# Last output products cut in two around the probability transposes, and another order of the small steps at the two layer borders

## The chip, the cores and the metric

The kernel runs on one core of a Trainium2 chip. The metric is the device time of one execution in microseconds (us). The core's engines are named as in the profile: PE is TensorE (PEld its weight loads), DVE is VectorE, ACT is ScalarE, POOL is GpSimd; SP issues most of the transfers, and its queue is written SPq.

## What is computed

Two blocks of a small network over 512 positions of width 1024. The first block runs two layers over 16 + 512 rows; `l` is 0 or 1.

```python
for l in range(2):
    a, g, zc, q, k, v, za, qi, ki, wi = split(h @ w_in[l])
    y_conv = gated depthwise convolution of (a, g), layer norm, silu, times silu(zc)
    y_attn = attention over the 132 keys that score best by (qi, ki, wi), times silu(za)
    y = concat(y_conv, y_attn) @ w_out[l]
    h = layer_norm(ALPHA * h + y) * post_ln_g[l] + post_ln_b[l]
x = rmsnorm(h, norm_gain)            # second block: one layer
q, k, v, gate_a, u, v_in, gate_b, merge = split(x @ w_in_2)
...                                  # attention, gated MLP, merge, output product, last norm
```

## The kernel before

**Numbers.** Every large product is made of three passes over a high and a low part: `x_hi` times `w_hi`, `x_lo` times `w_hi`, `x_hi` times `w_lo`. ACT makes a high part by a copy that rounds; a low part is what the rounding left. Low parts of the activations are subtractions on DVE (`x_lo(l, t)` for row tile t) or on POOL (`part_low`); low parts of the weights come by ACT and an accumulating transfer that POOL issues (`split_lo`), or, for the blocks in `LO_BY_POOL`, by two subtractions on POOL (`subtract_hi`, one for each half of the block).

**Weights.** They stream in blocks of 128x2048 through a ring of four buffers. SP loads block n when the last product that uses block n-4 has been made; then ACT splits it, then its low part is made. In the second block the ring's order is kv, q (two blocks), vin (two blocks), u (two), and so on: vin's second block takes kv's place, so its load waits for the last kv product, `("kv", 3)`.

**Rows.** Tiles 0 (16 rows) and 1 to 4 (128 rows each). In a layer's attention PE takes pairs of heads in turn, tile by tile; item i is one tile and one head. For each item PE transposes the probabilities (`turn_probs`, into one bank of `psum_A`, its last 16 keys into `psum_B` for tile 4), ACT copies them out (`take_probs_t`), and PE multiplies them by v (`probs_times_v`). Other work is put between these by tables: `OUTPUT_AT` names the items at which the output product of a finished tile is made (24 matmuls: 12 for the convolution half, 12 for the attention half), `POST_AT` those at which its layer norm is made.

**Border.** After the last item PE makes the output product of tile 4 in four parts (its two column halves `n`, the convolution half by `output_conv`, the attention half by `output_attn`) and, between them, transposes the finished tiles for the next layer (`turn_rows`). The norm of tile 4 runs last: DVE `residual(l, 1, 4)`, `aggregate`, then POOL `ln_deviation`, then DVE `post_norm`. After layer 1 comes the input norm of the second block as well: ACT squares the rows, POOL `input_deviation`, DVE `second_input(t)` scales them into `h_normed`, PE `turn_rows(1, t)` transposes them, ACT `x_hi` and DVE `x_lo` take them. The second block starts with the products `("kv", t)` (24 matmuls of 256 columns) and the halves `("q", t, half)` (12 matmuls of 512 columns), in the order of `KV_AND_Q`; `x_ready(1, t + 1)` makes `("kv", t)` wait for `x_lo(1, t + 1)`. Each engine works its instructions in the order in which they are written.

Of the kernel before, what the change touches and what calls it, by code (L numbers as in the profile page):

```python
# [26 lines left out]
P = 128  # L27
D = 1024
# [211 lines left out]
def gate_needed(l, name, t):  # L240
# [21 lines left out]
OUTPUT_CONV_AT = {0: 38, 1: 30}  # L262
# [6 lines left out]
KV_AND_Q = (("kv", 0), ("kv", 1), ("kv", 2), ("q", 0, 0), ("kv", 3), ("q", 1, 0), ("q", 2, 0), ("q", 3, 0),  # L269
# [27 lines left out]
def attention_extras(l):  # L297
# [51 lines left out]
    todo["pe"][OUTPUT_CONV_AT[l]].append(("wo conv", 0))  # L349
# [36 lines left out]
def build(nc, io, counted):  # L386

    with ExitStack() as ctx:
# [69 lines left out]
        hn = [sb("h_normed0", [P, D], at=K_AT + 4 * D), sb("h_normed1", [P, D], at=where[0])]  # L458
# [690 lines left out]
        def _(pool):  # L1149
            def subtract_hi(n):  # L1150

                for half in range(2):
# [65 lines left out]
            for l in range(DEPTH):  # L1218
# [55 lines left out]
                subtract_hi(after + 1)  # L1274
                ln_deviation((l, "post", 4), 4, P)
                split_lo(after + 2)
# [48 lines left out]
        def _(pe):  # L1325
# [229 lines left out]
            def output_half(l, n, half, t, ps):  # L1555
# [6 lines left out]
                for kk in range(4):  # L1562
# [15 lines left out]
            def output_conv(l, n):  # L1578
                buf, at = OUTPUT_BANK[n]
                ps = claim((l, "wo", n, 4), buf, (at,))[:, 0, :]  # L1580
                output_half(l, n, 0, 4, ps).then_inc(psum_full.mark((l, "wo", n, 4, "conv")), 1)
# [8 lines left out]
            for l in range(DEPTH):  # L1590
# [76 lines left out]
                def woven(i):  # L1667
                    for op in todo[i]:
# [8 lines left out]
                        elif op[0] == "wo":  # L1677
                            output_rows(l, *op[1:])
                        else:
                            output_conv(l, *op[1:])  # L1680
# [3 lines left out]
                for i in range(0, n, 2):  # L1684
# [7 lines left out]
                    woven(i + 1)  # L1692
                probs_times_v(l, n - 2)
# [110 lines left out]
            for name, t, *half in KV_AND_Q:  # L1804
                if name == "kv":
# [3 lines left out]
                    if t == 2:  # L1809
                        turn_rows(1, 4)  # L1810
                else:
                    query_half(t, *half)
            turn["AB"] = 1
# [44 lines left out]
        def _(dve):  # L1858
# [290 lines left out]
            for l in range(DEPTH):  # L2149
# [43 lines left out]
                for i in range(0, n, 2):  # L2193
# [12 lines left out]
                    woven(i + 1)  # L2206
                y_part(l, "attn", 4)

                if l < DEPTH - 1:
                    x_lo(l, 0)  # L2210
                    x_lo(l, 1)
                else:
                    second_input(1)
                    second_input(2)
                    x_lo(l, 1)
                    second_input(3)
                    x_lo(l, 2)
                residual(l, 0, 4)
                if l < DEPTH - 1:
                    x_lo(l, 2)  # L2220
                x_lo(l, 3)
# [3 lines left out]
                if l == DEPTH - 1:  # L2225
                    second_input(4)
                x_lo(l, 4)
# [339 lines left out]
```

## Time and profile before

| | |
|---|---|
| median of 3 runs | 1025.12 us (1024.62 to 1025.96) |
| the profiled execution | 1024.52 us, of it the span of the trace 1022.6 us |
| PE busy | 987.3 us, 97% of the span |
| DVE, ACT, POOL busy | 667.8, 558.8 and 231.4 us |
| mean granted clock of TensorE | 0.993 of full speed |

The span runs from the first to the last instruction. PE's busy time is nearly all of it; what is left to gain by order alone is the time in which PE waits, and a wait that another work covers costs nothing. The profile names for each wait the instruction that ended it.

### The profile page before, as it was taken

How to read it: one execution, taken by the hardware profiler on the slowest of the kernel's cores; microseconds unless marked ns; L12 is line 12 of the kernel's file. 1: busy time of each engine (PE TensorE's matmuls, PEld its weight loads, DVE VectorE, ACT ScalarE, POOL GpSimd, SP SyncE). 2: the span in 40 equal slices, each digit the busy share in tenths (PEclk: the TensorE clock that was granted, in tenths of full speed). 3: DMA queues.
4: the chain of work that ended last, by engine and by line, in shares of the span. 5: the costliest groups of instructions: out<-in, count | busy, mean ns of one | idle time of the engine just before them, and what ended most of it. 6: DMA issues, size and time to landing. Idle time of an engine off the chain costs nothing.

```text
span 1022.6 us, 15789 instructions
## 1 busy us (share of the span) xinstructions
PE 987.3 (97%) x6084; PEld 816.8 (80%) x6084; DVE 667.8 (65%) x1439; ACT 558.8 (55%) x915; POOL 231.4 (23%) x250
## 2 busy tenths in 40 slices
PE   7999999998999999999999999999999999999997
PEld 7888988886677988888778677888888788888886
DVE  3899999888674489999988756638422333333432
ACT  6685891645333558588165534544646566564442
POOL 0110771115211401077111512634101000000001
PEclk9999999999999999999999899999999999999999
DMA  8876874752001577488464400577777536365662
GB/s 301 196 180 179 210 181 131 166 124 83 1 1 50 157 177 176 124 185 187 124 171 79 156 21 1 171 180 188 176 210 197 114 89 158 90 158 126 175 155 82
DMA packets 23098, 143.92 MB, mean 141 GB/s; under 512 B 2785, under 2 KB 3297, under 8 KB 7281
## 3 DMA queue, kind: packets, MB, share of 16 engines
q0 software_dynamic: 8496, 60.36, 31.7%
q1 hardware_dynamic: 14528, 82.55, 22.8%
q8 instruction: 49, 0.80, 0.3%
q14 instruction: 25, 0.20, 0.1%
HBM read 140.81 MB, written 2.10 MB: 140 GB/s over the span
## 4 chain that ended last, share of the span: by engine, by line
PE 81%; ACT 7%; DVE 5%; DMA 3%; POOL 2%; issue 2%; SPq 0%; POOLq 0%; DVEq 0%; ACTq 0%
PE psum_B L1371 21%; PE psum_A L1371 14%; PE psum_B L1406 7%; PE psum_A L1406 7%; PE psum_A L1568 6%; PE psum_C L1448 3%; PE psum_A L1786 2%; PE psum_B L1568 2%; PE psum_B L1786 2%; PE psum_A L1484 2%; PE psum_B L1512 2%; DVE conv_acc L1887 2%; POOL w_lo L1155 2%; PE psum_B L1773 2%; PE psum_C L1371 1%
## 5 line engine op out<-in xcount | busy, mean ns | idle before, releaser
L1162 POOL DMA_DIRECT2D w_lo<-in_weights x59 | 52.0, 881 | 562.2 <-ACT w_lo L706 536.0
L1887 DVE SCALAR_TENSOR_TENSOR conv_acc<-u,vec,conv_acc 128x528 f32<-128x528 f32 (+1 forms) x240 | 172.3, 755 | 3.2
L1371 PE MATMUL psum_B<-x_hi,w_hi 128*128 128x264 f32 (+3 forms) x472 | 143.9, 338 | 2.5 <-DVE mlp_lo L2341 1.2
L1371 PE MATMUL psum_B<-x_lo,w_hi 128*128 128x264 f32 (+3 forms) x472 | 141.7, 333 | 0.0
L1371 PE MATMUL psum_B<-x_hi,w_lo 128*128 128x264 f32 (+3 forms) x472 | 141.2, 332 | 0.0
L705 ACT ACTIVATE w_hi<-w_raw 128x2048 fp32r<-128x2048 f32 (+2 forms) x73 | 113.4, 1553 | 18.7 <-DMA w_raw<-in_weights 18.2
L1371 PE MATMUL psum_A<-x_hi,w_hi 128*128 128x264 f32 (+3 forms) x408 | 111.1, 311 | 2.0 <-DVE za L2041 0.9
L706 ACT ACTIVATE w_lo<-w_raw 128x2048 fp32r<-128x2048 f32 (+2 forms) x73 | 112.7, 1544 | 0.0
L1371 PE MATMUL psum_A<-x_lo,w_hi 128*128 128x264 f32 (+3 forms) x408 | 109.1, 306 | 0.0
L1371 PE MATMUL psum_A<-x_hi,w_lo 128*128 128x264 f32 (+3 forms) x408 | 109.0, 305 | 0.0
L1371 PEld LDWEIGHTS psum_B<-x_hi,w_hi 128*128 128x128 f32 (+1 forms) x472 | 82.1, 186 | 13.4 <-issue 3.7
L1371 PEld LDWEIGHTS psum_B<-x_hi,w_lo 128*128 128x128 f32 (+1 forms) x472 | 82.0, 187 | 8.9
L1371 PEld LDWEIGHTS psum_B<-x_lo,w_hi 128*128 128x128 f32 (+1 forms) x472 | 82.0, 186 | 8.2
L1371 PEld LDWEIGHTS psum_A<-x_hi,w_hi 128*128 128x128 f32 (+1 forms) x408 | 70.0, 186 | 7.9 <-issue 3.1
L1371 PEld LDWEIGHTS psum_A<-x_hi,w_lo 128*128 128x128 f32 (+1 forms) x408 | 70.0, 186 | 3.4
L1371 PEld LDWEIGHTS psum_A<-x_lo,w_hi 128*128 128x128 f32 (+1 forms) x408 | 70.0, 186 | 3.4
L1946 DVE MATCH_REPLACE8 score<-top,score 128x528 f32<-128x528 f32 (+2 forms) x102 | 56.0, 557 | 0.0
L1937 DVE MAX8 top<-score 128x8 f32<-128x528 f32 (+2 forms) x102 | 51.6, 560 | 1.2 <-POOL score L1231 1.2
L1406 PE MATMUL psum_A<-w_hi,x_hi 128*128 128x512 f32 (+1 forms) x128 | 49.0, 383 | 0.5 <-ACT shifted L764 0.4
L1406 PE MATMUL psum_B<-w_hi,x_hi 128*128 128x512 f32 (+1 forms) x128 | 48.9, 382 | 0.4 <-ACT shifted L764 0.4
L1406 PE MATMUL psum_B<-w_hi,x_lo 128*128 128x512 f32 (+1 forms) x128 | 48.7, 380 | 0.0
L1406 PE MATMUL psum_A<-w_hi,x_lo 128*128 128x512 f32 (+1 forms) x128 | 48.7, 380 | 0.0
(407 smaller groups left out, 2199.5 us busy)
## 6 DMA issues: line engine op xcount, KB each, us to landing
w_raw<-in_weights SPq DMA_DIRECT2D x66, 1024.0 KB, 5.0
w_lo<-in_weights POOLq DMA_DIRECT2D x57, 1024.0 KB, 8.6
h<-in_x SPq DMA_DIRECT2D x1, 2048.0 KB, 11.0
out<-h SPq DMA_DIRECT2D x4, 512.0 KB, 2.6
x_first<-in_x_t SPq DMA_DIRECT2D x3, 528.0 KB, 8.3
post_ln_g<-in_post_ln_g SPq DMA_DIRECT2D x2, 512.0 KB, 4.7
post_ln_b<-in_post_ln_b SPq DMA_DIRECT2D x2, 512.0 KB, 6.1
w_raw<-in_weights SPq DMA_DIRECT2D x2, 288.0 KB, 6.4
```

The source lines that it names most:

```text
L705: act.activation(whi[n % RING][:, a:b], raw[n % RING][:, a:b], ACT.Copy)
L706: got = act.activation(wlo[n % RING][:, a:b], raw[n % RING][:, a:b], ACT.Copy, scale=-1.0)
L1155: pool.tensor_tensor(wlo[n % RING][:, a:b], raw[n % RING][:, a:b], whi[n % RING][:, a:b].bitcast(F32), ALU.subtract).then_inc(pool_lo.mark ...
L1162: pool.dma_start(wlo[n % RING][:, 0:width], io["weights"][n, :, 0:width], accum_op=ALU.add) \
L1371: mm = pe.matmul(ps[0:cols, i, 0:b - a], w[wp][:, kt, at:at + cols], x[xp][:, kt, a:b], start=(kt == 0 and wp + xp == 0), stop=(kt == KD - ...
L1406: mm = pe.matmul(ps[:, 0, 0:width], act_parts[xp][:, kt, c0:c0 + P], w[wp][:, kk, at:at + width], start=(kt == 0 and wp + xp == 0), stop=( ...
L1448: mm = pe.matmul(banks[odd][0:SIZE[t], i, 0:b - a], qs[s:s + HD, hd // 2, START[t]:END[t]], ks_of[s:s + HD, a:b], start=True, stop=True)
L1568: mm = pe.matmul(ps, x[xp][:, kt, START[t]:START[t] + P], w[wp][:, kk, 0:DC], start=(kt == 0 and wp + xp == 0), stop=(kt == KD - 1 and wp ...
L1786: mm = pe.matmul(ps[:, 0, :], w[wp][:, kt, d % 4 * P:d % 4 * P + P], parts[xp][:, kt, :], start=(kt == 0 and wp + xp == 0), stop=(kt == CT ...
L1887: got = dve.scalar_tensor_tensor(dst, src, w, dst, ALU.mult, ALU.add)
L1937: dve.max(top8[:, t - 1, :], vals).then_inc(topk_max.mark((l, r, t)), 1)
L1946: dve.match_replace(vals, top8[:, t - 1, :], vals, MARK).then_inc(topk_marked.mark((l, r, t)), 1)
```

## The change

Three edits, none of which adds or takes away arithmetic; the POOL subtraction of one weight block is issued as two separate steps with another step between them.

1. In the last four items of each layer's attention, the output product of tile 3's second column half, 24 matmuls in one piece before, is made in two pieces of 12, one on each side of a probability transpose, and the product `wo conv 0` of tile 4, 12 matmuls in one piece before, in two pieces of 6 around the last one.
2. At both borders DVE makes the low part of tile 3 (`x_lo(l, 3)`), and after layer 1 that of tile 2 too, later in its order; `residual` and the norm of tile 4 come ahead. POOL makes the deviation for tile 4 between the two halves of the second weight block. After layer 1 the scaled inputs of tiles 1 and 2 (`second_input`) come ahead of the last gated attention tile (`y_part`), for which `h_normed` is given other memory (that of `k`).
3. In `KV_AND_Q`, `("kv", 3)` goes behind two more query halves, and the transpose of tile 4 behind `("q", 0, 0)` instead of behind `("kv", 2)`.

```diff
-        (34, 0, 3, "A"), (36, 1, 3, "A")),
+        (34, 0, 3, "A")),
...
-OUTPUT_CONV_AT = {0: 38, 1: 30}
+LAST_OUTPUT_AT = {0: 36, 1: 28}
...
-KV_AND_Q = (("kv", 0), ("kv", 1), ("kv", 2), ("q", 0, 0), ("kv", 3), ("q", 1, 0), ("q", 2, 0), ("q", 3, 0),
+KV_AND_Q = (("kv", 0), ("kv", 1), ("kv", 2), ("q", 0, 0), ("q", 1, 0), ("q", 2, 0), ("kv", 3), ("q", 3, 0),
...
-    todo["pe"][OUTPUT_CONV_AT[l]].append(("wo conv", 0))
+    i = LAST_OUTPUT_AT[l]
+    todo["pe"][i].append(("wo rows", 0, 1, 3, "A"))
+    todo["pe"][i + 1].append(("wo rows", 1, 1, 3, "A"))
+    todo["dve"][i + 1].append(("residual", 1, 3))
+    todo["pe"][i + 2].append(("wo conv", 0, 0, 2))
+    todo["pe"][i + 3].append(("wo conv", 0, 2, 4))
...
-        hn = [sb("h_normed0", [P, D], at=K_AT + 4 * D), sb("h_normed1", [P, D], at=where[0])]
+        hn = [sb(f"h_normed{i}", [P, D], at=K_AT + 4 * D * i) for i in range(2)]
...
-            def subtract_hi(n):
+            def subtract_hi(n, parts=(0, 1)):
 
-                for half in range(2):
+                for half in parts:
...
                 subtract_hi(after)
-                subtract_hi(after + 1)
+                subtract_hi(after + 1, (0,))
                 ln_deviation((l, "post", 4), 4, P)
+                subtract_hi(after + 1, (1,))
                 split_lo(after + 2)
...
+            def output_part(l, half, n, t, buf):
+
+                use = (l, "wo", n, t)
+                ps = (bank[buf][:, 1:2, :] if half else claim(use, buf, (1,)))[:, 0, :]
+                mm = output_half(l, n, half, t, ps)
+                if half:
+                    mm.then_inc(psum_full.mark(use), 1)
...
-                    if t == 2:
-                        turn_rows(1, 4)
                 else:
                     query_half(t, *half)
+                    if (t, *half) == (0, 0):
+                        turn_rows(1, 4)
...
+                if l == DEPTH - 1:
+                    second_input(1)
+                    second_input(2)
                 y_part(l, "attn", 4)
 
                 if l < DEPTH - 1:
                     x_lo(l, 0)
-                    x_lo(l, 1)
                 else:
-                    second_input(1)
-                    second_input(2)
-                    x_lo(l, 1)
                     second_input(3)
-                    x_lo(l, 2)
+                x_lo(l, 1)
                 residual(l, 0, 4)
-                if l < DEPTH - 1:
-                    x_lo(l, 2)
-                x_lo(l, 3)
+                x_lo(l, 2)
                 residual(l, 1, 4)
                 aggregate(l, 4)
                 post_norm(l, 4)
                 if l == DEPTH - 1:
                     second_input(4)
+                x_lo(l, 3)
                 x_lo(l, 4)
```

The order of instructions shows it at three places; the line numbers in the rows of the change are its own. First PE, at the last probability transpose of layer 1 (`exps_124` are the probabilities, `w_hi_51` and `w_lo_59` the weights of `wo conv 0`), before:

```order
L1568 MATMUL psum_A<-w_hi_51,x_hi 128x512
L1568 MATMUL psum_A<-w_hi_51,x_lo 128x512
L1568 MATMUL psum_A<-w_lo_59,x_hi 128x512
L1484 MATMUL psum_A<-ident,exps_124 128x128 x4
L1490 MATMUL psum_B<-ident,exps_124 16x64
L1512 MATMUL psum_B<-probs_t_113,v 64x128
```

and with the change:

```order
L1577 MATMUL psum_A<-w_hi_51,x_hi 128x512
L1577 MATMUL psum_A<-w_hi_51,x_lo 128x512
L1577 MATMUL psum_A<-w_lo_59,x_hi 128x512
L1493 MATMUL psum_A<-ident,exps_124 128x128 x4
L1499 MATMUL psum_B<-ident,exps_124 16x64
L1577 MATMUL psum_A<-w_hi_51,x_hi 128x512
L1577 MATMUL psum_A<-w_hi_51,x_lo 128x512
L1577 MATMUL psum_A<-w_lo_59,x_hi 128x512
```

Six of the product's matmuls now stand between the transpose and the first product with v; the other places of this kind look the same.

Second DVE, at the border to the second block, from the first residual of tile 4 on (tile 3 stands in `psum_D`, tiles 2 and 4 in `psum_C`), before:

```order
L2080 SCALAR_TENSOR_TENSOR h<-h,psum_A 128x512
L2088 BN_STATS stats<-h 128x6
L2127 TENSOR_TENSOR x_lo<-psum_D,x_hi 128x8x128
L2080 SCALAR_TENSOR_TENSOR h<-h,psum_B 128x512
L2088 BN_STATS stats<-h 128x6
L2093 BN_AGGR meanvar<-stats 128x2
L2103 SCALAR_TENSOR_TENSOR h<-h,meanvar,post_ln_g 128x1024
L2107 SCALAR_TENSOR_TENSOR h<-h,rstd,post_ln_b 128x1024
L2119 SCALAR_TENSOR_TENSOR h_normed_99<-h,rstd,norm_gain 128x1024
L2127 TENSOR_TENSOR x_lo<-psum_C,x_hi 128x8x128
```

and with the change:

```order
L2102 SCALAR_TENSOR_TENSOR h<-h,psum_A 128x512
L2110 BN_STATS stats<-h 128x6
L2149 TENSOR_TENSOR x_lo<-psum_C,x_hi 128x8x128
L2102 SCALAR_TENSOR_TENSOR h<-h,psum_B 128x512
L2110 BN_STATS stats<-h 128x6
L2115 BN_AGGR meanvar<-stats 128x2
L2125 SCALAR_TENSOR_TENSOR h<-h,meanvar,post_ln_g 128x1024
L2129 SCALAR_TENSOR_TENSOR h<-h,rstd,post_ln_b 128x1024
L2141 SCALAR_TENSOR_TENSOR h_normed_99<-h,rstd,norm_gain 128x1024
L2149 TENSOR_TENSOR x_lo<-psum_D,x_hi 128x8x128
L2149 TENSOR_TENSOR x_lo<-psum_C,x_hi 128x8x128
```

The low part of tile 3, from `psum_D`, moved from ahead of the second residual to behind the scaled input of tile 4.

Third POOL, at the same border (`w_lo_59` is kv's low part, `w_lo_60` that of the first query block, `w_lo_57` that of the second), before:

```order
L1155 TENSOR_TENSOR w_lo_59<-w_raw_55,w_hi_51 128x1024 x2
L1155 TENSOR_TENSOR w_lo_60<-w_raw_56,w_hi_52 128x1024 x2
L1171 TENSOR_SCALAR var_eps<-meanvar 128x1
L1174 TENSOR_TENSOR rstd<-var_eps,minus_half 128x1
L1162 DMA w_lo_57<-in_weights 128x2048
L1171 TENSOR_SCALAR var_eps<-prob_sums 128x1
```

and with the change:

```order
L1163 TENSOR_TENSOR w_lo_59<-w_raw_55,w_hi_51 128x1024 x2
L1163 TENSOR_TENSOR w_lo_60<-w_raw_56,w_hi_52 128x1024
L1179 TENSOR_SCALAR var_eps<-meanvar 128x1
L1182 TENSOR_TENSOR rstd<-var_eps,minus_half 128x1
L1163 TENSOR_TENSOR w_lo_60<-w_raw_56,w_hi_52 128x1024
L1170 DMA w_lo_57<-in_weights 128x2048
L1179 TENSOR_SCALAR var_eps<-prob_sums 128x1
```

The second half of the query block's subtraction moved behind the first deviation, and so ahead of the transfer and of the second deviation (`var_eps<-prob_sums`), which still stand behind it.

## Rows read from the trace of the kernel before

**Rows 1.** The page, busy time, share of the span and instructions of each engine

```profile
PE 987.3 (97%) x6084; PEld 816.8 (80%) x6084; DVE 667.8 (65%) x1439; ACT 558.8 (55%) x915; POOL 231.4 (23%) x250
```

**Rows 2.** Timeline of PE: start us, us, instruction [idle before, its releaser]

```profile
319.30 0.63 PE L1484 MATMUL psum_A<-ident,exps 128*128 128x128 f32 x4 [0.83 <-ACT probs_t L846]
...
325.85 0.33 PE L1512 MATMUL psum_B<-probs_t,v 128*64 128x128 f32 x2 [0.78 <-ACT probs_t_meta L846]
...
649.28 1.07 PE L1552 MATMUL psum_C<-ident,h_normed 128*128 128x128 f32 x8 [0.54 <-DVE h_normed L2119]
```

**Rows 3.** Timelines of POOL, DVE and PE at the first border

```profile
337.69 4.78 POOL L1155 TENSOR_TENSOR w_lo<-w_raw,w_hi 128x1024 fp32r<-128x1024 f32 x2 [2.52 <-ACT w_hi L702]
342.55 1.11 POOL L1171 TENSOR_SCALAR var_eps<-meanvar 128x1 f32<-128x1 f32 x1
...
339.50 1.23 DVE L2127 TENSOR_TENSOR x_lo<-psum_C,x_hi 128x1024 fp32r<-128x1024 f32 x1 [1.58 <-ACT x_hi L889]
...
344.41 1.28 DVE L2107 SCALAR_TENSOR_TENSOR h<-h,rstd,post_ln_b 128x1024 f32<-128x1024 f32 x1 [0.80 <-POOL rstd L1174]
...
345.84 1.07 PE L1552 MATMUL psum_D<-ident,h 128*128 128x128 f32 x8 [0.77 <-DVE h L2107]
```

**Rows 4.** Timeline of DVE at the second border

```profile
650.09 1.23 DVE L2127 TENSOR_TENSOR x_lo<-psum_D,x_hi 128x1024 fp32r<-128x1024 f32 x1 [0.95 <-ACT x_hi L889]
...
656.86 0.68 DVE L2080 SCALAR_TENSOR_TENSOR h<-h,psum_B 128x512 f32<-128x512 f32 x1
...
658.30 0.21 DVE L2093 BATCH_NORM_AGGREGATE meanvar<-stats 128x2 f32<-128x12 f32 x1
...
661.38 1.28 DVE L2107 SCALAR_TENSOR_TENSOR h<-h,rstd,post_ln_b 128x1024 f32<-128x1024 f32 x1 [0.80 <-POOL rstd L1174]
664.97 1.28 DVE L2119 SCALAR_TENSOR_TENSOR h_normed<-h,rstd,norm_gain 128x1024 f32<-128x1024 f32 x1 [2.30 <-POOL rstd L1174]
```

**Rows 5.** Timelines of POOL and ACT at the second border

```profile
648.28 11.21 POOL L1155 TENSOR_TENSOR w_lo<-w_raw,w_hi 128x1024 fp32r<-128x1024 f32 x4 [0.23 <-ACT w_hi L702]
659.58 1.05 POOL L1171 TENSOR_SCALAR var_eps<-meanvar 128x1 f32<-128x1 f32 x1
...
662.06 0.91 POOL L1162 DMA_DIRECT2D w_lo<-in_weights  x1 [0.80 <-ACT w_lo L706]
663.95 0.18 POOL L1171 TENSOR_SCALAR var_eps<-prob_sums 128x1 f32<-128x1 f32 x1 [0.97 <-ACT square L899]
...
662.70 1.06 ACT L899 ACTIVATE square<-h 128x1024 f32<-128x1024 f32 x1 [0.99 <-DVE h L2107]
```

**Rows 6.** Timeline of PE at the second border: first kv matmul, transpose of tile 4

```profile
656.62 0.28 PE L1406 MATMUL psum_A<-w_hi,x_hi 128*128 128x256 f32 x1
...
666.40 1.06 PE L1552 MATMUL psum_C<-ident,h_normed 128*128 128x128 f32 x8 [1.12 <-DVE h_normed L2119]
```

**Rows 7.** Chain that ended last: start us, us, what (a whole kv product)

```profile
670.25 2.82 PE psum_B L1406 x24
```

**Rows 8.** Timelines around vin's second weight block, and vin's first matmul

```profile
673.10 0.33 SPq L618 DMA_DIRECT2D w_raw<-in_weights  x1
...
681.70 1.92 ACT L705 ACTIVATE w_hi<-w_raw 128x2048 fp32r<-128x2048 f32 x1 [8.15 <-DMA w_raw<-in_weights]
...
685.78 0.91 POOL L1162 DMA_DIRECT2D w_lo<-in_weights  x1 [8.08 <-ACT w_lo L706]
...
692.36 0.40 PE L1406 MATMUL psum_A<-w_hi,x_hi 128*128 128x512 f32 x1
```

**Rows 9.** Transfers issued from 685.6 to 698: count, KB, median us to landing

```profile
w_lo<-in_weights POOLq DMA_DIRECT2D x1, 1024.0 KB, 7.9
```

**Rows 10.** Stretches: length, busy PE, PEld, DVE, ACT, POOL, PEclk, DMA share, GB/s

```profile
577.00:582.00 5.00, 5.00 (x16) 3.21 (x17) 4.89 (x14) 2.49 (x7) 1.12 (x4) 0.50 0.68 223
1016.00:1019.00 3.00, 0.46 (x2) 0.02 (x1) 1.44 (x3) 0.85 (x3) 0.74 (x2) 1.00 0.06 23
1019.00:1020.00 1.00, 0.00 (x0) 0.00 (x0) 0.43 (x1) 0.59 (x1) 0.00 (x0) 0.54 0.00 0
```

More of the change, by code:

```diff
@@ L253 @@
     0: ((17, 0, 0, "A"), (19, 0, 1, "B"), (22, 1, 0, "A"), (25, 1, 1, "B"), (27, 0, 2, "A"), (29, 1, 2, "A"),
[2 rows of a table removed]
+        (34, 0, 3, "A")),
+    1: ((17, 0, 1, "A"), (19, 0, 2, "B"), (21, 1, 1, "A"), (23, 1, 2, "A"), (26, 0, 3, "A")),
 }
@@ L1553, in turn_rows, with output_half @@
                 mm.then_inc(psum_full.mark(use), 1)
-            def output_half(l, n, half, t, ps):
+            def output_half(l, n, half, t, ps, kks=range(4)):
                 part = ("conv", "attn")[half]
@@ L1561, in output_half @@
                     pe.wait_ge(meta_paired.sem, meta_paired.at((l, part)))
-                for kk in range(4):
+                for kk in kks:
                     kt = half * 4 + kk
@@ L1576, in output_rows, with output_conv @@
                 output_half(l, n, 1, t, ps).then_inc(psum_full.mark(use), 1)
-            def output_conv(l, n):
+            def output_part(l, half, n, t, buf):
[4 more added lines that the diff above has]
+                    mm.then_inc(psum_full.mark(use), 1)
+            def output_conv(l, n, first=0, last=4):
                 buf, at = OUTPUT_BANK[n]
-                ps = claim((l, "wo", n, 4), buf, (at,))[:, 0, :]
-                output_half(l, n, 0, 4, ps).then_inc(psum_full.mark((l, "wo", n, 4, "conv")), 1)
+                ps = (bank[buf][:, at:at + 1, :] if first else claim((l, "wo", n, 4), buf, (at,)))[:, 0, :]
+                mm = output_half(l, n, 0, 4, ps, range(first, last))
+                if last == 4:
+                    mm.then_inc(psum_full.mark((l, "wo", n, 4, "conv")), 1)
             def output_attn(l, n):
@@ L1678, in woven @@
                             output_rows(l, *op[1:])
+                        elif op[0] == "wo rows":
+                            output_part(l, *op[1:])
                         else:
```

1 row of the table OUTPUT_AT is left out of this document.

## Prediction

> **What bounds the kernel now.** I read the page first: PE is busy 987.3 us of a span of 1022.6 [rows 1], so only its waits, some 35 us, can be won by another order, and a new wait of PE is paid in full wherever PE has no later idle time to give it up in. Then the waits of PE near the edits, in its timeline. At the last item of a layer's attention PE transposes probabilities, and the next transpose or product waits until ACT has copied them out: 0.83 us at 319.30, 0.78 at 325.85 [rows 2]; the same pair stands in layer 1, so there are four such waits. The transpose of tile 2 waits 0.54 for DVE's `h_normed` [rows 2], the transpose of tile 4 at the first border 0.77 for the norm [rows 3], and at the second border 1.12 for `h_normed` of tile 4 [rows 6]. These waits are what the edits can take away. Against them stands what the moved steps released before: whom did `x_lo(1, 3)` and `("kv", 3)` let go, and when? Those I read from the timelines of DVE, POOL and SP at the second border.
>
> **Edit 1, pieces around the transposes.** No matmul is added. After each of these transposes PE now has 12 matmuls or 6 of them; the shorter piece, at the kv block's rate of 2.82 us for 24 narrower matmuls [rows 7] no faster than 0.7 us and by its doubled columns about 1.4, covers waits of 0.83 and 0.78. Gain 4 x 0.8 = 3.2 us, half in each layer. What the pieces wait for (bank, probabilities) was there long before. Bounds: 2.6 if pieces restart slowly, 3.2.
>
> **Edit 2 at the first border.** `x_lo(0, 3)`, 1.23 us, stood ahead of the second residual, and POOL's deviation started at 342.55 only after both halves of the subtraction, 4.78 us from 337.69 [rows 3]. With both out of the way the norm of tile 4 comes up to 1.3 us earlier, and the 0.77 us of PE's wait goes. The delayed second half of the weight subtraction (2.4 us, half of 4.78) now starts after the deviation, at about the same distance to its user; it may cost up to 0.5. I take 0.7. Bounds 0.2 to 0.9.
>
> **Edit 2 at the second border, the start.** The scaled inputs of tiles 1 and 2 come while DVE idles, and the 0.54 of [rows 2] goes. But the transpose of tile 3 needs `x_lo(1, 1)`, which ended at 651.32 [rows 4], and that hangs on ACT and on kv's weights, whose load starts no earlier. PE would reach it at about 651, so little is left of it: I take 0.05, bounds 0 to 0.5. With edit 1 the last product of tile 4 ends 1.65 us earlier in layer 1's own time.
>
> **Edit 2 at the second border, the new wait.** `("kv", 2)` waits for `x_lo(1, 3)`, which now stands behind `second_input(4)`. When is that? Before, the second residual started at 656.86 and the aggregate ended at 658.51 [rows 4]; the deviation started at 659.58, 1.07 late, behind POOL's subtractions (four in 11.21 us, 2.8 each) [rows 5]. Now the residual starts at 656.86 - 1.65 = 655.2, the aggregate ends at 656.9, three subtractions end at 648.28 + 8.4 = 656.7. Deviation and root took 661.38 - 659.58 = 1.8 with the way to DVE [rows 4, 5], so the norm's last step runs 658.7 to 660.0 and the square ends at 661.2. POOL meanwhile makes the fourth subtraction, 658.6 to 661.4, and issues the transfer, 0.91 [rows 5], to 662.4; then the second deviation, 664.97 - 663.95 = 1.0, to 663.4: the 1.2 us that POOL's order costs here cancels the 1.07 won. `second_input(4)` 1.28 to 664.7, `x_lo(1, 3)` 1.23 to 665.95, PE at 666.0. PE is ready for `("kv", 2)` after two kv products: 656.62 - 1.65 + 2 x 2.82 = 660.6 [rows 6, 7]. So it waits 5.4 us, in place of 1.12 at the transpose of tile 4, which is now long ready. Bounds: 4.2 (POOL never in the way) to 6.2.
>
> **Edit 3, the ring.** `("kv", 3)` moves behind two query halves more (the transpose of tile 4 stays ahead of it). Seven query halves took 692.36 - 673.07 = 19.3 us after it, 2.76 each [rows 7, 8]. SP issued the load of vin's second block when it was done, 673.10; ACT split it at 681.70, POOL issued the low part at 685.78, and it landed 7.9 later, 693.7 [rows 8, 9]: 20.6 us after `("kv", 3)`. The first vin product needs it for its second half, 2.8 us after its start: 22.1 after `("kv", 3)`, so 1.5 to spare. With the change only five query halves follow: 13.8 + 2.8 = 16.6, and the low part is 4.0 us late. Nothing behind it gives this back: the loads that follow hang on PE's own products. Bounds 0.5 (the load, 8.6 us beside another, as if alone by 3.5 faster) to 7 (the low part beside the loads that the last query half lets go).
>
> **The clock.** In this trace, with TensorE idle from 1016.5, the granted clock was still 1.00 until 1019 and 0.54 in the next microsecond; from 577 to 582, after sparse work, it stood at 0.50, the lower level of 1.2 GHz, with PE busy all 5 us [rows 10]. A wait of 5.4 us is longer than that idle stretch. Work at half speed for 5 us costs 2.5; I take 2.0 for the kv wait, bounds 0 and 2.5, and none for the 4.0 us wait, in which the forecast is near even. The Trainium skill, TensorE: Matmul & The Clock Gate, section "HAM oscillation — how this bites in real kernels", says that a TensorE left waiting for a transfer is throttled back and works its next matmuls cold, every time. By that rule both new waits would cost it, and the sum would be 2.0 us higher; the trace agrees with the fall after idling, and no row shows one after a wait of PE of 4 us inside the kernel.
>
> **The sum**, against the profiled execution's 1024.52: -3.2 (transposes), -0.7, -0.05, +5.4 - 1.1 (kv wait for the tile 4 wait), +2.0 (clock), +4.0 (vin) = +6.35; 1030.9. The median of the runs is 0.6 above that execution: 1031.5.
>
> **The rivals.**
> - The clock falls at the vin wait too: 1033.5. For it: 4.0 us of idling against some 3 at the end [rows 10]. Against: PE works 12 matmuls just before. 20%.
> - The clock never falls: 1029.5. For it: the three rows are all there is, and none shows a fall after one long wait inside the kernel. Against: the kv wait is almost twice the idle stretch at the end. 12%.
> - Only the kv wait is real, because vin's low part lands in time: 1025.5 to 1027.5 with the clock's share. It needs the 20.6 us chain to shrink to 16.6; the contended load could give 3.5. 14%.
> - Faster: `x_lo(1, 3)` is there when PE asks. Then 3.2 + 0.75 + 1.1 are won and vin's wait must be absent too: 1020. It decides at 660.6: if the chain from the residual to `x_lo(1, 3)` took under 5.5 us instead of 10.8. Its DVE and ACT steps alone (0.68, 0.69, 0.21, 1.28, 1.06, 1.28, 1.23) take 6.4. 6%, mostly for an error of mine in who waits for whom.
>
> **How the numbers follow.** My forecast, both waits and one fall of the clock, has 40%, its own range 1029 to 1034. The rest, 8%, are other costs of either sign. The range for 8 in 10 is 1026.8 to 1035: it leaves out the faster case, part of the third, and the high tail of the vin wait with a second fall. A measurement of this kernel tells about 0.2% from no change, 2.05 us. Faster 7%, the same 8% (the lower half of the third rival and some of the rest), slower 85%.
>
> **What would show it.** In the changed kernel's trace: no wait on `probs_t` before the last transposes and products of each layer; none before the transpose of tile 4 at the first border; on PE a wait of 4 to 6 us ahead of the third kv product that ends with `x_lo`; a PEclk near 0.5 just after it; a wait of 2.5 to 5 us in the middle of the first vin product that ends with the transfer into `w_lo`; from there to the end the same durations as before. I am wrong if the kv wait is under 3 us, if the vin product runs through, or if later waits of PE shrink and give the time back.

## The result and the profile after

The changed kernel takes 1038.53 us (median; 1035.53 to 1040.48) against 1024.87 us of the kernel before: a ratio of 1.0127, 95% interval 1.0115 to 1.0139, or 13.7 us slower. The forecast was 1031.5 us, and its range ended at 1035.0. The profiled execution, at 1035.53 us the shortest of the four, is 11.0 us above that of before.

The page's busy row answers to [rows 1]; columns as there.

```profile
span 1033.5 us, 15791 instructions
## 1 busy us (share of the span) xinstructions
PE 990.4 (96%) x6084; PEld 819.2 (79%) x6084; DVE 670.3 (65%) x1439; ACT 558.3 (54%) x915; POOL 229.2 (22%) x250
```

PE has the same 6084 matmuls and is busy 3.1 us longer; the other 7.8 us of the longer span are time in which it waits. The waits of PE around the two borders, 318 to 360 and 640 to 715 us (who waits, for whom, sum, number, longest):

```profile
PE psum_D L1561 <- DVE h L2129: 1.5, 1, 1.5
PE psum_C L1561 <- DVE x_lo L2149: 0.7, 1, 0.7
...
PE psum_A L1415 <- DVE x_lo L2149: 6.2, 1, 6.2
PE psum_A L1415 <- DMA w_lo<-in_weights: 3.4, 1, 3.4
PE psum_D L1561 <- DVE x_lo L2149: 1.3, 1, 1.3
```

The waits on `probs_t` (two of them in [rows 2]) are gone. The first row is the 0.77 of [rows 3], grown to 1.48 where the forecast had it vanish; the two of 0.7 and 1.3 on `x_lo` are new and were not forecast; the kv wait of 6.2 and the wait of 3.4 for vin's `w_lo` are the two that were.

The first border after, DVE, POOL and PE (timelines; they answer to [rows 3]):

```profile
340.07 1.28 DVE L2125 SCALAR_TENSOR_TENSOR h<-h,meanvar,post_ln_g 128x1024 f32<-128x1024 f32 x1
342.15 3.32 DVE L2129 SCALAR_TENSOR_TENSOR h<-h,rstd,post_ln_b 128x1024 f32<-128x1024 f32 x1 [0.80 <-POOL rstd L1182]
...
340.12 1.28 POOL L1179 TENSOR_SCALAR var_eps<-meanvar 128x1 f32<-128x1 f32 x1 [1.83 <-DVE meanvar L2115]
341.49 0.55 POOL L1182 TENSOR_TENSOR rstd<-var_eps,minus_half 128x1 f32<-128x1 f32 x1
342.00 2.39 POOL L1163 TENSOR_TENSOR w_lo<-w_raw,w_hi 128x1024 fp32r<-128x1024 f32 x1
...
345.62 1.06 PE L1561 MATMUL psum_D<-ident,h 128*128 128x128 f32 x8 [1.48 <-DVE h L2129]
```

POOL's deviation now starts 2.43 us earlier than in [rows 3] (340.12 for 342.55), as the edit means it to, and the norm's last step on DVE 2.26 earlier. But this step, 1.28 us in [rows 3], shows 3.32, and it ends 1.08 behind the subtraction half that POOL began just before it (342.00 + 2.39 = 344.39, 345.47). The step ends where it ended before, and PE's transpose of tile 4 starts at 345.62 for 345.84.

The second border after, DVE, POOL and PE (they answer to [rows 4 to 6]):

```profile
659.88 3.32 DVE L2129 SCALAR_TENSOR_TENSOR h<-h,rstd,post_ln_b 128x1024 f32<-128x1024 f32 x1 [0.79 <-POOL rstd L1182]
665.50 1.28 DVE L2141 SCALAR_TENSOR_TENSOR h_normed<-h,rstd,norm_gain 128x1024 f32<-128x1024 f32 x1 [2.30 <-POOL rstd L1182]
666.70 1.21 DVE L2149 TENSOR_TENSOR x_lo<-psum_D,x_hi 128x1024 fp32r<-128x1024 f32 x1
...
657.85 1.28 POOL L1179 TENSOR_SCALAR var_eps<-meanvar 128x1 f32<-128x1 f32 x1 [1.65 <-DVE meanvar L2115]
...
659.73 2.38 POOL L1163 TENSOR_TENSOR w_lo<-w_raw,w_hi 128x1024 fp32r<-128x1024 f32 x1
...
655.90 0.28 PE L1415 MATMUL psum_A<-w_hi,x_hi 128*128 128x256 f32 x1
...
667.97 0.58 PE L1415 MATMUL psum_A<-w_hi,x_hi 128*128 128x256 f32 x1 [6.25 <-DVE x_lo L2149]
```

The same pair stands here: 3.32 us beside POOL's 2.38. The kv block starts only 0.72 before that of [rows 6], and its third product waits 6.25.

Vin's second block (timelines of ACT, POOL and PE, as [rows 8]):

```profile
691.61 1.92 ACT L713 ACTIVATE w_hi<-w_raw 128x2048 fp32r<-128x2048 f32 x1 [6.71 <-DMA w_raw<-in_weights]
...
695.69 0.91 POOL L1170 DMA_DIRECT2D w_lo<-in_weights  x1 [9.10 <-ACT w_lo L714]
...
698.16 0.39 PE L1415 MATMUL psum_A<-w_hi,x_hi 128*128 128x512 f32 x1
...
704.53 0.50 PE L1415 MATMUL psum_A<-w_hi,x_hi 128*128 128x512 f32 x1 [3.44 <-DMA w_lo<-in_weights]
...
708.99 0.39 PE L1415 MATMUL psum_B<-w_hi,x_hi 128*128 128x512 f32 x1
```

SP issued the load at 684.45, when `("kv", 3)` was done; the low part was there at 704.5, 20.1 later. And the clock (stretches, columns as [rows 10]):

```profile
664.00:665.00 1.00, 0.00 (x0) 0.00 (x0) 0.00 (x0) 1.00 (x6) 0.44 (x2) 0.52 0.61 98
...
668.00:672.00 4.00, 4.00 (x23) 4.00 (x24) 0.00 (x0) 0.00 (x0) 0.00 (x0) 0.64 0.93 304
672.00:675.00 3.00, 3.00 (x17) 2.44 (x16) 0.00 (x0) 0.45 (x2) 0.00 (x0) 1.00 0.03 12
702.00:705.00 3.00, 0.47 (x2) 0.42 (x3) 2.93 (x12) 0.00 (x0) 2.83 (x3) 1.00 0.94 330
705.00:708.00 3.00, 3.00 (x9) 2.31 (x8) 2.96 (x9) 0.00 (x0) 1.10 (x1) 0.50 0.99 421
```

The granted clock, the seventh number, is at 0.5, the level of 1.2 GHz, from about 664 on, with PE idle since 661.7, and again from 705, just behind the wait of 3.44 us. It costs 1.41 at the kv product (667.97 to the next product at 672.20 is 4.23, against 2.82 in [rows 7]; the lower level began while PE still stood, so over half of it cost nothing) and 1.68 at vin (12 matmuls in 708.99 - 704.53 = 4.46, against 2.78, half of a vin product of before).

The 10.9 us by which the span is longer, by place, as the shift of PE's starts against before, in the two profiled executions:

| PE reaches | before | after | shift | change |
|---|---|---|---|---|
| the product behind layer 0's last transposes | 327.29 | 325.42 | -1.87 | -1.87 |
| layer 1's first block behind tile 4's transpose | 346.66 | 346.66 | 0 | +1.87 |
| transposes of tile 1, second border | 647.71 | 646.23 | -1.48 | -1.48 |
| transposes of tile 2 | 649.28 | 647.10 | -2.18 | -0.70 |
| first kv product | 656.62 | 655.90 | -0.72 | +1.46 |
| third kv product | 662.28 | 667.97 | +5.69 | +6.41 |
| first vin product | 692.36 | 698.16 | +5.80 | +0.11 |
| second vin product | 697.92 | 708.99 | +11.07 | +5.27 |
| the end | 1022.6 | 1033.5 | +10.9 | -0.2 |

Not all of the first -1.87 is the change's. At 300 us, ahead of every edited place, PE is already 0.38 early: before, the granted clock is at 0.50 from 242 to 244 us, and in this execution it is at 1.00 there. The pieces around the transposes give the other 1.5.

### The profile page after: what moved, and what is told of

The parts are those of the page before. It is cut to its first block, busy times and chain, and to the rows that moved or that the text cites. A ratio compares the mean times of both kernels' runs of the same rounds, so it can differ in the third digit from the quotient of the medians.

```text
span 1033.5 us, 15791 instructions
## 1 busy us (share of the span) xinstructions
PE 990.4 (96%) x6084; PEld 819.2 (79%) x6084; DVE 670.3 (65%) x1439; ACT 558.3 (54%) x915; POOL 229.2 (22%) x250
## 4 chain that ended last, share of the span: by engine, by line
PE 81%; ACT 7%; DVE 6%; DMA 4%; issue 2%; POOL 0%; POOLq 0%; SPq 0%; DVEq 0%; ACTq 0%
PE psum_B L1380 21%; PE psum_A L1380 14%; PE psum_A L1415 8%; PE psum_B L1415 8%; PE psum_A L1577 6%; DMA w_raw<-in_weights 3%; PE psum_C L1457 2%; PE psum_B L1577 2%; PE psum_A L1808 2%; PE psum_B L1808 2%; DVE conv_acc L1909 2%; PE psum_A L1493 2%; PE psum_B L1521 2%; PE psum_B L1795 1%; PE psum_C L1380 1%
## 5 line engine op out<-in xcount | busy, mean ns | idle before, releaser
L1415 PE MATMUL psum_A<-w_lo,x_hi 128*128 128x512 f32 (+1 forms) x128 | 49.7, 388 | 0.0
```

What stands on the lines that cost most here:

```text
L1415: mm = pe.matmul(ps[:, 0, 0:width], act_parts[xp][:, kt, c0:c0 + P], w[wp][:, kk, at:at + width], start=(kt == 0 and wp + xp == 0), stop=( ...
```

## The experiments

Two theories of the miss stood at first. One: both forecast waits are there, a little larger, the clock falls at each, and POOL's new order costs what the transposes give. The rival: the waits forecast are the smaller part, and the loss is in transfers that come late and a clock that falls elsewhere. All ratios are to the kernel before on the same chip.

**The same kernel again.**

> The changed kernel once more, unaltered, for a second trace. Its four runs spread from 1035.53 to 1040.48 us with a granted clock of 0.990 down to 0.987. Theory A (the spread is the clock: after the two long waits of TensorE the lower level lasts for a different time in each run): the kv wait (6.2 us in the first trace) and the vin wait (3.4 us) are within 1 us of the first trace, and a time above 1036.5 comes with more microseconds at PEclk 0.50 behind them. Theory B (the spread is in transfers): the vin wait itself differs by 2 us or more.

1040.34 us (1039.15 to 1043.54), ratio 1.0153 (1.0133 to 1.0173). Its trace (1039.15) has the same kv wait, 6.25, and a wait for vin's low part of 5.15 in place of 3.44. The load was issued at 686.30, when `("kv", 3)` was done, and the product went on at 708.39, 22.1 us later, for 20.1 in the first trace. The vin wait differs by 1.7, so neither theory is met in full, and the trace has a share of each. Its span is 3.8 us longer: 1.8 of it come at the vin product, most of that the later transfer, 0.6 ahead of the kv block, and most of the rest with the clock. PE's busy time and granted clock there (length, PE busy, PEclk, DMA share, GB/s):

```profile
668.00:672.00 4.00, 3.43 (x16) 0.50 0.97 288
672.00:675.00 3.00, 3.00 (x14) 0.61 0.25 96
```

The kv wait ends at 668.57 here, and the lower level lasts to 674.3, where in the first trace it was over at 670.9, 2.9 after the wait's end: the kv product takes 5.28 instead of 4.23. The executions of this kernel spread over 8 us (1035.5 to 1043.5), those of before over 4.3 (1023.54 to 1027.83). Both the transfer and the place of the clock's fall have a part in that; how much of the 8 us each has, two traces can't show.

**POOL's order undone.** POOL again makes both halves, then the deviation.

```diff
-                subtract_hi(after + 1, (0,))
+                subtract_hi(after + 1)
                 ln_deviation((l, "post", 4), 4, P)
-                subtract_hi(after + 1, (1,))
```

> The change with POOL's order put back: both halves of the second block's subtraction ahead of the deviation for tile 4. Theory A (POOL's second half beside the norm's last step on DVE holds that step up, 3.32 us in place of 1.28, at both borders): the step is back at 1.28 in both places, the wait for it at the first border falls from 1.5 us to under 0.3, the kv wait from 6.2 to about 5, and the kernel is 2.5 to 3 us faster than the change (about 1035.5 beside 1038.5). Theory B (the prediction's: the order of POOL is neutral, the deviation would wait for the subtraction instead): within 1 us of the change.

1036.21 us (1033.94 to 1037.88), ratio 1.0101 (1.0084 to 1.0118), 4.1 us below the changed kernel on the same chip, where theory A gave 2.5 to 3. The norm's last step takes 1.28 at both borders, PE's wait for it at the first is gone, and the kv wait is 4.81 instead of 6.25. The norm's first step (L2124), which now runs in part beside POOL's last half, takes 1.68 and 1.87 instead of 1.28. The vin wait is 5.12 in this trace, so part of the gain went there.

**The place of `x_lo(1, 3)` undone**, ahead of the second residual as before, the rest of the change kept.

```diff
                 x_lo(l, 2)
+                if l == DEPTH - 1:
+                    x_lo(l, 3)
                 residual(l, 1, 4)
...
-                x_lo(l, 3)
+                else:
+                    x_lo(l, 3)
```

> The change with one step of DVE put back: after layer 1 the low part of tile 3 comes ahead of the second residual of tile 4 again. Theory A (the third kv product waits for it, and the clock falls in that wait): no wait of TensorE before the third kv product, none or under 0.5 us before the transpose of tile 4, no stretch at PEclk 0.50 there; the vin wait of 3.4 us stays, with a fall of the clock. 7 to 8 us faster than the change, some 1030.5. Theory B (that wait only takes the place of one for the scaled input of tile 4): a wait of over 3 us ahead of the transpose of tile 4 instead, and under 4 us faster.

1030.18 us (1027.43 to 1031.05), ratio 1.0039 (1.0025 to 1.0052): 10.2 us below the changed kernel, where theory A gave 7 to 8. No kv wait. The vin wait stands, 3.40 us, and the clock falls behind it.

**`KV_AND_Q` and the transpose of tile 4 undone**, the rest kept.

```diff
-KV_AND_Q = (("kv", 0), ("kv", 1), ("kv", 2), ("q", 0, 0), ("q", 1, 0), ("q", 2, 0), ("kv", 3), ("q", 3, 0),
+KV_AND_Q = (("kv", 0), ("kv", 1), ("kv", 2), ("q", 0, 0), ("kv", 3), ("q", 1, 0), ("q", 2, 0), ("q", 3, 0),
...
+                    if t == 2:
+                        turn_rows(1, 4)
...
-                    if (t, *half) == (0, 0):
-                        turn_rows(1, 4)
```

> The change with the order of kv and query products put back (the fourth kv product two query halves earlier, tile 4's transpose behind the third kv product). Theory A (the load of vin's second block hangs on the fourth kv product): the vin wait of 3.4 us is gone with the fall of the clock behind it, the kv wait of 6.2 us stays; 4.5 to 6 us faster than the change, some 1033. Theory B (the low part is late because the whole border is late and its transfer collides with others): a vin wait of over 2 us stays.

1031.79 us (1029.70 to 1033.13), ratio 1.0057 (1.0040 to 1.0075): 8.6 us below the changed kernel, where theory A gave 4.5 to 6. The vin wait is gone; the kv wait is 6.25 as before, with the clock's fall. So each forecast wait has its own cause, and either edit taken back removes its own. Both parts of the change that were forecast to lose do lose. All three runs gained more than theory A said. The three differences are against the changed kernel's second measurement, 1.0153; its first was 1.0127, so each is uncertain by 2.7 us.

**All three undone**: POOL's order, `x_lo(1, 3)`, `KV_AND_Q`. Left are the pieces around the transposes, `x_lo(0, 3)` behind the norm, and the scaled inputs ahead of the last gated tile.

> The changed kernel with three parts undone: the POOL order of the weight subtraction, the place of x_lo(1, 3) (again ahead of the second residual), and the place of ("kv", 3) with the transpose of tile 4. Kept: the pieces around the transposes, x_lo(0, 3) behind the norm, the second block's inputs ahead of the last gated tile. Theory A (each undone part made its own wait, and nothing else is in the change): no kv wait, no vin wait, no step of the norm above 2.3 us, the four transposes' waits gone; 1020.5 to 1022.5 against 1025.9. Theory B (what the transposes give is only moved to the next border, where POOL and DVE are the later ones): 1024 to 1026, with PE's waits for h or x_lo at the borders larger by what the transposes won.

1023.39 us (1021.88 to 1025.57), ratio 0.9987 (0.9978 to 0.9996), and later, measured anew,

> The best version so far once more, on the same chip as the one with the transpose of tile 4 moved. Theory A: 0.9978 to 0.9996 of before again, and 0.5 to 1 us above the one with the transpose moved. Theory B (the small gain was chance): within 0.1% of before.

1023.29 us (1021.58 to 1024.89), ratio 0.9981 (0.9972 to 0.9990). This version beats both kernels; it is 1.9 and 1.7 us faster than before, less than theory A gave it and more than B. Its waits at the second border, of the first of the two traces:

```profile
PE psum_D L1560 <- DVE x_lo L2148: 1.4, 1, 1.4
PE psum_C L1560 <- DVE h_normed L2140: 0.9, 1, 0.9
```

The 1.4 is the wait for `x_lo` of tile 1: PE is ready for the transpose of tile 3 that much ahead of ACT and DVE.

**The pieces around the transposes alone**, added to the kernel before.

> The kernel before with the pieces around the transposes alone. Theory A: 3 us less, 1022.9; the waits for the norm at the two borders stay near 0.8 and 1.1. Theory B (PE comes earlier to borders whose chain starts at POOL's or ACT's weight work and does not come earlier): the waits at the borders grow by 1 to 1.5 each and the kernel gains 0 to 1 us.

1026.35 us (1022.92 to 1031.00), ratio 1.0013 (1.0002 to 1.0025). Theory B, and more: the edit forecast at -3.2 is worth nothing by itself. The trace is of the longest execution (1031.0), so it shows how the edit can lose, and not what it does in the median. Its DVE and PE at the second border:

```profile
653.44 1.23 DVE L2148 TENSOR_TENSOR x_lo<-psum_D,x_hi 128x1024 fp32r<-128x1024 f32 x1 [4.65 <-ACT x_hi L897]
654.58 2.82 DVE L2140 SCALAR_TENSOR_TENSOR h_normed<-h,rstd,norm_gain 128x1024 f32<-128x1024 f32 x1
...
657.55 1.72 PE L1560 MATMUL psum_D<-ident,h_normed 128*128 128x128 f32 x7 [4.76 <-DVE h_normed L2140]
```

DVE stood 4.65 us for `x_hi`, which ACT made only at 652.41, behind two weight steps (650.50) that had waited 4.45 for their transfer. Then `h_normed` of tile 3, behind `x_lo(1, 1)` in the old DVE order, took 2.82 for 1.28, beside a subtraction of POOL (653.98 to 656.32). PE waited 4.76, and the clock fell. In the changed kernel `second_input(3)` is ahead of `x_lo(1, 1)`, and this wait is not there. How often it comes I can't say from one trace; the twelve executions lie from 1022.9 to 1031.0.

**POOL's order alone**, added to the kernel before.

> The kernel before with POOL's order alone: the deviation of tile 4 between the two halves of the last weight subtraction. Theory A (a POOL subtraction that runs beside a step of the norm on DVE holds that step until it ends, and the split puts one beside the norm's last step): the last step takes 3.3 us instead of 1.28 at both borders, its start comes 1 us earlier at most; PE's wait at the borders grows by 0.7 to 1.3 each, so 1 to 2.5 us slower, 1027 to 1028.4. Theory B (the order is neutral, as the forecast had it): within 0.5 us of before.

1032.05 us (1026.92 to 1033.44), ratio 1.0056 (1.0036 to 1.0075): 6.8 us slower, far more than theory A gave it. In its trace, the shortest execution (1026.92), the norm's last step takes 3.28 and 3.34, and PE waits 2.77 for it at the first border (0.77 in [rows 3]) and 2.65 for `h_normed` at the second (1.12 in [rows 6]). The steps are as theory A has them, and the two waits together 3.5 longer. The six executions are two at 1027 (mean granted clock 0.996) and four at 1032 to 1033.4 (0.990 to 0.991). The two groups differ by what a clock lower by 0.005 to 0.006 of full speed costs in 1030 us, 5 to 6 us by estimate; against before, at 0.994 in its median, the lower clock would be 3 to 4 of the 6.8 and the waits the rest. That is worked out from the mean clocks; the next run was for a trace of it.

> The kernel before with POOL's order alone once more, for a trace. Its six executions lay at 1027 (two, mean granted clock 0.996) and 1032 (four, 0.990 to 0.991). Theory A (a wait of PE of 2.6 to 2.8 at a border brings the clock down in most executions): if this one is near 1032, the granted clock falls to 0.5 within or just behind the waits of the two borders, some 2.5 us of products lost at each. Theory B (the slower ones have longer waits, by a transfer that comes late): no fall at the borders, and the waits of PE there sum to 10 or more instead of 6.

1029.23 us, one execution, mean clock 0.994: between the two groups. The steps and the wait of the first border are the same to 0.05 us. At the second border the wait was 2.39, and behind it the clock is down (PE's busy time and granted clock by stretch):

```profile
664.00:667.00 3.00, 3.00 (x28) 1.00 0.42 44
667.00:670.00 3.00, 0.61 (x6) 1.00 0.85 167
670.00:673.00 3.00, 3.00 (x13) 0.56 0.94 228
```

In the first trace the same stretches stand at 1.00 behind a wait of 2.65. So a wait of 2.4 to 2.8 us brings the clock down in some executions and not in others, and the length alone does not decide. That both borders fall in the executions at 1032 I did not see: no trace fell on one. Theory B's later transfers are not in either trace. The clock also falls far from both borders, and not in every execution: from 242 to 244 us it is below full speed in ten of the fourteen traces of this text, and near 525 us (0.50 from 524 to 526, in one trace from 527 to 530) in five. So the four at 1032 may owe something to falls elsewhere too.

**The changed kernel with two undone**, POOL's order kept.

> The changed kernel with the place of x_lo(1, 3) and the place of ("kv", 3) undone, POOL's order kept. Theory A (two waits and the clock's fall beside them are nearly all of the loss): no kv wait and no vin wait, 1022.5 to 1025, and above the kernel that has POOL's order undone too by 1 to 2.5. Theory B (some of the loss is in the steps kept, the other order of the inputs of the second block among them): above 1026.

1029.09 us (1024.66 to 1030.94), ratio 1.0033 (1.0017 to 1.0049). That is 5.7 us above the version that has POOL's order undone too, where theory A gave 1 to 2.5; and its median is above the 1026 that theory B named, but for another reason than B's, since the steps kept stand in the best version as well. Its trace has the waits of 1.41 for `h` at the first border and 2.35 for `h_normed` at the second (none and 0.89 in the best version), and a clock of 0.50 to 0.70 from 667 to 670.

**The same subtraction, but not beside the norm.** POOL's order as in the split, and the last half waits until the norm of tile 4 is made.

```diff
                 subtract_hi(after + 1, (0,))
                 ln_deviation((l, "post", 4), 4, P)
+                pool.wait_ge(normed.sem, normed.at((l, "x" if l < DEPTH - 1 else "h", 4)))
                 subtract_hi(after + 1, (1,))
```

> The kernel before with POOL's order as in the split, and POOL's last subtraction half held back until the last step of the norm of tile 4 has ended. Theory A (a subtraction of POOL beside a step of the norm on DVE holds the step): that step takes 1.28 at both borders, PE's wait at the first border 0.8 or less, at the second 1.1 to 2.2, since the second deviation of tile 4 now stands behind the half; no run near 1032; 1023.5 to 1026.5. Theory B (the step is long for another reason, its start beside ACT's or PE's work): it still takes 3.3, and the time is that of the split, 1027 to 1033.

The norm's last step at both borders on DVE, and POOL's halves behind it:

```profile
345.79 1.28 DVE L2109 SCALAR_TENSOR_TENSOR h<-h,rstd,post_ln_b 128x1024 f32<-128x1024 f32 x1 [0.79 <-POOL rstd L1174]
...
663.75 1.28 DVE L2109 SCALAR_TENSOR_TENSOR h<-h,rstd,post_ln_b 128x1024 f32<-128x1024 f32 x1 [0.80 <-POOL rstd L1174]
...
347.15 2.35 POOL L1155 TENSOR_TENSOR w_lo<-w_raw,w_hi 128x1024 fp32r<-128x1024 f32 x1 [1.48 <-DVE h L2109]
...
665.12 2.40 POOL L1155 TENSOR_TENSOR w_lo<-w_raw,w_hi 128x1024 fp32r<-128x1024 f32 x1 [1.48 <-DVE h L2109]
```

1.28, not 3.3, with everything else as in the split: the subtraction beside it is what makes the step long. That part of theory A is shown. Its time is not: 1027.71 us (1026.40 to 1031.66), ratio 1.0025 (1.0014 to 1.0035), still slower than before, though 0.3% below the split (1.0056), some 3 us. The trace is of the longest execution. The late half is late for its own user: PE waits 1.36 for POOL's `w_lo` at the first border, and 2.76 at the second for `h_normed`, since the deviation stands behind the half and its transfer.

**The transpose of tile 4 behind the first query half**, in the best version; `("kv", 3)` stays.

> The best version so far (POOL's order, x_lo(1, 3) and ("kv", 3) as before) with the transpose of tile 4 behind the first query half instead of ahead of it; ("kv", 3) stays where it was. Theory A: the wait of 0.9 for the inputs of tile 4 goes and nothing starts later: 0.5 to 1 us less than without it, 1022 to 1023 against 1025.3. Theory B (the transpose then comes with less room ahead of the last query half, or the place is as good): no difference from the version without it.

1026.02 us (1022.97 to 1028.88), ratio 1.0003 (0.9991 to 1.0016), 2.7 above the version without it on the same chip. Neither theory: the wait of 0.9 is gone, and a new one of 2.37 stands at `("kv", 3)`, for `x_lo` of tile 4, since that product reads the tile just transposed. I had not looked at what `("kv", 3)` reads. It would also be a reason why the change moved both together.

## Why the prediction missed

The direction, the two new waits and what they wait for were right; the sum was 4.7 us short of the profiled execution (6.35 for 11.0). By place, forecast and measured: up to the first kv product -3.95 and -0.72; the kv wait with the clock's fall, less the wait for tile 4, +6.3 and +6.5; the vin product +4.0 and +5.3; behind it 0 and -0.2. Step by step:

**Edit 1, -3.2: nearly right where it stands, and given back at the next border.** The four waits are gone, worth 1.5 in layer 0 (-0.38 to -1.87) and 1.5 in layer 1 (0 to -1.48). By the first kv product PE is ahead by 0.72, where the sum had -3.2 - 0.7 - 0.05 = -3.95. This is the step that failed most, 3.2 us: "Gain 4 x 0.8 = 3.2 us" took every microsecond won ahead of a border through it. The borders end in chains of ACT, DVE and POOL, and these chains didn't start earlier: PE waits 0.72 and 1.26 for `x_lo`, which it had not waited for before. The edit alone, in the kernel before, brought nothing (1.0013).

Why the chain did not start earlier stands in the chains that ended last (start, us, what), before and then after, at the second border:

```profile
642.05 5.06 DMA w_raw<-in_weights
647.14 1.07 ACT w_hi L702
...
640.36 1.61 PE psum_A L1577 x6
641.99 5.94 DMA w_raw<-in_weights
647.95 2.01 ACT w_hi L710 x2
```

ACT makes the high part of that weight block ahead of `x_hi` of tile 1, and `x_lo` follows that. SP issues the block's load when `wo conv 0` is done (`psum_full` of that product, in the kernel). The edit moved the last six matmuls of just this product behind the transpose, so although PE was 0.86 early at 640 us, the load started 0.06 earlier; then it took 0.9 longer, and ACT's step came 0.81 later than before. The forecast had looked at what the pieces wait for, and not at what waits for them. It had even named this load ("starts no earlier") as a limit on edit 2, at 0.05 us, and not as one on edit 1. The trace with `x_lo(1, 3)` undone bears it out: there the load took 5.07 us, PE waited 0.39 for this `x_lo` instead of 1.26, and the first kv product stood 1.8 ahead of before. Why the load takes 5.1 us in some traces and 5.9 and more in most of those with the pieces is not shown, and no run moved the load alone.

**POOL's order at the first border, "it may cost up to 0.5", and at the second, "cancels the 1.07 won": wrong mechanism.** I counted POOL's queue and not what POOL's work does to DVE's. The norm's last step took 3.32 instead of 1.28 at both borders, beside POOL's half; without that neighbour it took 1.28. So the 0.7 won at the first border was a wait grown from 0.77 to 1.48, and at the second the kv wait is 6.25 with POOL's order and 4.81 without it. In the kernel before the same thing stood in rows that I had read past, the norm's first step at the first and at the second border, and a subtraction of POOL:

```profile
342.33 1.28 DVE L2103 SCALAR_TENSOR_TENSOR h<-h,meanvar,post_ln_g 128x1024 f32<-128x1024 f32 x1
658.54 2.04 DVE L2103 SCALAR_TENSOR_TENSOR h<-h,meanvar,post_ln_g 128x1024 f32<-128x1024 f32 x1
651.34 3.43 POOL L1155 TENSOR_TENSOR w_lo<-w_raw,w_hi 128x1024 fp32r<-128x1024 f32 x1
```

The step of 2.04 runs beside the end of POOL's 11.21 us [rows 5]. The subtraction of 3.43 began 0.11 behind DVE's `h_normed` step of 1.28 (651.23). The forecast took "2.8 each" for the four subtractions and 2.4 for the same step at the first border, and did not ask why they differ. The Trainium skill has the rule, in SBUF — State Buffer, section "Who interferes with whom": a VectorE instruction with two inputs in SBUF and a GpSimd instruction that reads SBUF exclude each other, and the one that starts second stands until the first is through. The traces agree (344.39 + 1.08 = 345.47), down to the step with one input in PSUM: `x_lo(1, 3)` in the best version's second trace takes 1.23 from 656.10, in the midst of POOL's subtractions (652.91 to 660.04). It should have been one of the rivals.

**The price of that.** By PE's waits alone POOL's order costs about 3.5; measured, it is 6.8 alone, 5.7 in the version with two undone and 4.1 in the changed kernel (2.7 against its first measurement), which has a long wait and a fallen clock at the second border in any case.

**The new kv wait, +5.4: the wait and its releaser right, the size in part by luck.** It is 6.25, just past the bound of 6.2. The forecast charged 1.2 us to POOL's queue, the fourth subtraction and the transfer ahead of the second deviation. That queue cost nothing: POOL was free at 662.94 and then stood 1.53 for ACT's square, which ended at 664.38. What cost was DVE's step, held by 2.04, and 2.04 for 1.2 is the excess of 0.85. With POOL's order undone the wait is 4.81. The wait of 1.12 for tile 4 is gone in exchange, as forecast.

**The ring, +4.0: right.** 3.44 in this trace, 5.15 in the next, 3.40 and 5.12 with other parts undone. Its 20.6 us chain, from SP's load to the second half of the vin product, measured 20.0 to 22.1 in the four traces. So the cause is shown and the 4.0 lies inside what they give.

**The clock, +2.0: right in kind, short by one fall.** At the kv wait 1.41 instead of 2.0 (1.5 to 2.5 in the other three traces that have this wait); at the vin wait 1.68, which the sum had at none and the first rival at 2.0. That rival was the right case, and in every trace with a vin wait (3.40, 3.44, 5.12, 5.15 us) the clock fell. That I gave it half the weight of the other was an error: the rows at the end of the kernel [rows 10] show a fall between 1019 and 1020 with TensorE idle from 1016.5, which is less than 4.0; and the text calls this fall "near even", while the rival has 20% beside 40%. The Trainium skill's rule in TensorE: Matmul & The Clock Gate, section "HAM oscillation — how this bites in real kernels", which I cited, agrees with these four and with the kv wait.

**What the two waits cost together.** From the version with two undone, `("kv", 3)` moved alone adds 0.1% (1.0033 to 1.0039), `x_lo(1, 3)` alone 0.2% (to 1.0057), both 0.9 to 1.2% (1.0127 and 1.0153). The intervals of the first three overlap, and they were measured on two chips, so 0.1 and 0.2% are not clear of noise; that both together cost far more than the two alone is. By the traces, each alone mostly takes the place of the wait of 2.35 for tile 4's inputs and of the clock's fall beside it; with both, the second finds nothing left to replace. In PE's starts: the second vin product stands at 700.56 with both undone, at 700.59 with only `("kv", 3)` moved, at 704.30 with only `x_lo` moved, and at 708.99 and 712.86 with both.

**The range** ended at 1035.0 because the highest case had one more fall and nothing for borders that give back or for transfers that swing. The medians lie 13.7 us apart, 2.7 more than the two profiled executions, since the one profiled here is the shortest of its four: with a wait on a transfer and two falls of the clock in it, one execution is a draw from a spread of 8 us. What stays open: what the clock does in the executions of POOL's order alone at 1032, how often the pieces alone meet the wait of 4.76, and why the load behind `wo conv 0` takes longer with them.

## What to carry to other kernels

A wait taken away ahead of a border is won only if the engines that end the border come earlier as well; before adding it to a sum, find the next wait of the same engine and ask what its releaser hangs on. When a product is cut in two, ask also who waits for its end: here a load did, and the cut put that end behind the time won. When a step is moved on GpSimd, read VectorE's row at its new time: two 128x1024 elementwise steps that both read twice from SBUF ran one after the other. And a wait of TensorE as long as those here, 3.4 us and more, is to be priced with a fall of the clock, 1.4 to 2.5 us each in these traces; one on a transfer with that transfer's spread as well.

## What the hardware showed that I had not expected

- DVE's 128x1024 step on two SBUF inputs took 1.28 us alone and 3.28 to 3.34 beside a POOL subtraction of 2.35 to 2.40 that had started 0.15 earlier. It works both ways: POOL's 128x1 step took 1.28 when it began 0.05 behind a DVE step of 1.28, and 0.18 (the deviation at 664.47, of the same shape) where DVE was idle. The profile shows the time stood still as busy time of the instruction, not as idle time before it, so no view of waits names it.
- The granted clock fell in or just behind waits of TensorE of 3.4 us and more in every trace that has one around the second border, and after waits of 2.35 to 2.76 there in three of five (not after 2.37 in the version with the transpose of tile 4 moved, nor after 2.65 in POOL's order alone). It cost least where it had fallen before the wait ended: the kv product behind the same wait of 6.25 took 4.23 us in one trace and 5.28 in the next.
